# Hybrid DiT layer on one core: three attentions in one stage, PSUM banks shared by hand, and loads and splits moved ahead

## The chip, the cores and the metric

The kernel is one program on one core of a Trainium2 chip. The metric is device time in microseconds (us); lower is better. Engines are named as in the profile: PE (TensorE matmul), PEld (its weight loads), DVE (VectorE), ACT (ScalarE), POOL (GpSimd), SP (SyncE, which here only issues transfers). SPq, ACTq and POOLq are the sequencers of those engines.

## What is computed

One layer (DEPTH 1) over 512 latent tokens and 256 context tokens, 768 together, D_MODEL 2048, all float32. Cut to what matters:

```python
hn_lat = rmsnorm(h, norm1_g) * (1 + sc1) + sh1      # 512 tokens; hn_ctx likewise, 256 tokens
pc, pl = split(hn_ctx @ w_in), split(hn_lat @ w_in) # q_lat 512, kv_lat 256, k_rope 64, mLSTM q k v o 768 each, gates 8 + 8, NA q k v 512 each
q = rope(rmsnorm(q_lat) @ w_uq); k = rope(rmsnorm(kv_lat) @ w_uk); v = rmsnorm(kv_lat) @ w_uv
mla = softmax(q k^T * scale) v                      # 6 heads, 128 + 64 wide, values 128
ml  = mlstm_bidirectional(...)                      # 4 heads of 192, both directions, exponential gates
na  = softmax(q k^T * scale + bias) v               # 4 heads of 128; neighbourhood of 8 x 16 plus the context
h = h + g1 * (concat(mla, ml, na) @ w_out)          # 768 + 768 + 512 = 2048
h = h + g2 * conv_ffn(rmsnorm(h) * (1 + sc2) + sh2) # w_up, depthwise conv of 3, silu gate, w_down
return rmsnorm(h, final_norm_g)
```

## The kernel before, in words

Four parts follow one another: `stage_front` (norms, modulation, the projection by `w_in` in 43 column tiles), `stage_mix` (the three attentions), and `stage_tail` (output projection and ConvFFN). Each `nc.Block` ends in a join: no engine begins the next block before all have left this one. `stage_mix` has four blocks in turn: the MLA projections, the MLA softmax, the mLSTM, and the NA softmax. The big products of front and tail are made in three passes over operands split into a high and a low half (`x_hi`, `x_lo`, `f_hi`, `f_lo`): ACT copies the high half (L1639, L1612), DVE subtracts for the low one (L1745, L1715), PE multiplies (L1844).

**MLA projections** (`stage_mla`, L793 to L1023). SP loads the latent of the queries and the two norm gains (L797 to L799), the gate biases (L802), then the latent of keys and values and the rope inputs; ACT issues the three weight loads, `w_uq` first (L842 to L844); POOL loads the gate rows (L829). ACT scales the query latent by the gain (L847, four instructions), and PE waits for all four before its first product (L1003). Beside that, DVE and ACT turn the gates into rows (L894 to L930) that SP stores to the DRAM tensors `rrow` and `em`; DVE then rotates the queries (L933).

**MLA softmax** (`softmax_heads`, 6 heads x 4 query tiles = 24 units, tag `a`). Unit u: PE scores it (L1030), DVE takes the maximum (L1136, L1138), ACT the exponential (L1183), DVE the inverse of its sum (L1144), POOL multiplies (L1157). Two units later PE transposes it (L1105), ACT and DVE copy it out of PSUM (L1166, L1118), and once a head is complete PE multiplies by the values (L1089) and ACT stores the head to the DRAM tensor `mix` (L1173, L1175). While this runs SP loads the mLSTM operands (`prefetch`).

**mLSTM** (`stage_mlstm`, 4 heads x 6 key tiles = 24 units, tag `g`). For each unit SP loads a row of weights, repeated over the partitions, into one of 5 ring slots (L1265), once the values product of five units earlier is done; POOL adds the causal mask for four tiles of six (L1283), ACT takes the exponential (L1334), PE scores two units ahead (L1426), DVE multiplies score by weight (L1366, L1371), and PE multiplies by the values (L1447). After a head, ACT reads the sums out of PSUM (L1344), DVE makes and inverts the denominators (L1383, L1387, L1392), PE spreads them over the partitions (L1456), DVE scales (L1400), POOL joins the two directions and gates them (L1290, L1292), SP stores to `mix` (L1254). For heads 0 to 2 that is spread over the units of the next head; for head 3 it stands at the end of the block. The ACT queue opens this block by issuing the operands of NA: queries, keys, values, the window and eight slabs of bias (L1312 to L1319); POOL adds the window to the slabs after its masks of head 0 (L1300).

**NA softmax** (`stage_na`, 16 units, tag `c`) is the same `softmax_heads`; here DVE adds the bias out of the slab (L1127, L1129) and finds the maximum (L1133).

**Tail** (`stage_tail`). SP loads tile 0 of `w_out` (L1564), all of `mix` (L1569, 4 MB), tile 1, the residual `h` (L1571, 4 MB) and the conv weights. ACT splits 16 blocks of `mix` and tile 0, DVE follows with the low halves; then DVE waits for `h` and only after it takes the low half of tile 1. Product 0 waits block by block for `x_lo`, product 1 for `f_lo` of tile 1.

PSUM is held by names: each block takes its own tiles and gives them back.

## Time and profile before

| | |
|---|---|
| median of 3 runs | 2904.06 us (2904.06, 2904.89, 2895.7) |
| profiled execution | 2902.73 us, span of its instructions 2901.1 us, mean granted clock 0.964 |
| PE busy | 2699.4 us, 93% of the span, 12122 matmuls |
| DVE, ACT, POOL busy | 1197.9, 741.8, 192.9 us |
| DMA | 371.13 MB, mean 128 GB/s |
| first PE instruction of the MLA projections | 721.42 us |
| first score of the mLSTM, first values | 968.90 us, 990.36 us |
| first score of NA | 1132.30 us |
| first load of the tail, first product | 1216.22 us, 1237.70 us |

A busy PE is not a PE at its peak: the clock granted to it is one of two levels, and at the lower one the same matmul takes twice as long while its busy time reads the same share. The time to look for is therefore idle PE and PE at a clock below 1.00. The stretch of this change is about a fifth of the span, from 702 us (the last product of the front) to 1252 us (the second tile of the tail).

### The profile page before, as it was taken

The page shows a single profiled execution, that of the slowest core. Times are in us where ns is not written, and L with a number is a line of the kernel's source. Part 1 is how long each engine was busy: PE and PEld are TensorE (multiplying, and loading weights), DVE is VectorE, ACT ScalarE, POOL GpSimd, SP SyncE. Part 2 cuts the span into 40 slices and gives each one's busy share as a digit, 9 for nine tenths or more (in the row PEclk, how much of TensorE's full clock was granted, in tenths as well). Part 3 has the DMA queues.
Part 4 walks back from the last instruction along what each step waited for, and adds up shares of the span by engine and source line. Part 5 has one row for each costly group of instructions (what it writes and reads, how often), then busy time and mean ns, then how long its engine had stood idle before and what let it go on. Part 6 is the DMA issues. An engine that isn't in the chain of part 4 may idle for free.

```text
span 2901.1 us, 31111 instructions
## 1 busy us (share of the span) xinstructions
PE 2699.4 (93%) x12122; PEld 2088.8 (72%) x12122; DVE 1197.9 (41%) x1220; ACT 741.8 (26%) x822; POOL 192.9 (7%) x195
## 2 busy tenths in 40 slices
PE   5999999997999696599899999999999999999996
PEld 3788888885534243278678888888888888888785
DVE  5535434651622155343544433344333433334334
ACT  3222112221223121232333321223212322223221
POOL 1000000001033223200000000000000000000000
PEclk9999999998979798899999999999999999999998
DMA  9765555863050520242222222222232222322222
GB/s 354 272 245 209 218 197 214 316 242 126 11 114 12 155 83 16 96 168 87 73 101 87 101 90 99 102 95 101 81 113 87 101 97 90 103 96 98 82 90 98
DMA packets 98923, 371.13 MB, mean 128 GB/s; under 512 B 21920, under 2 KB 35280, under 8 KB 68360
## 3 DMA queue, kind: packets, MB, share of 16 engines
...
q14 instruction: 22, 0.18, 0.0%
HBM read 347.53 MB, written 22.79 MB: 128 GB/s over the span
## 4 chain that ended last, share of the span: by engine, by line
PE 56%; DVE 1%; DMA 1%; issue 0%; ACT 0%; DVEq 0%; SPq 0%; ACTq 0%
PE f_ps L1844 55%; PE f_ps L1857 1%; DMA mix_under_u<-mix 1%; DVE h L1833 0%; DVE f_lo L1715 0%; ACT f_hi L1612 0%; DVE f_square_sum L1830 0%; PE f_pn L1871 0%; DVE h L1732 0%; DVE f_square_sum L1739 0%; ACT f_val L1618 0%; ACT x_hi L1639 0%; PE f_pn L1890 0%; ACT f_val L1631 0%; DVE f_val L1726 0%
## 5 line engine op out<-in xcount | busy, mean ns | idle before, releaser
L1844 PE MATMUL f_ps<-x_hi,f_hi 128*128 128x512 f32 x1632 | 637.1, 390 | 29.1 <-DVE f_lo L1715 29.1
L1844 PE MATMUL f_ps<-x_lo,f_hi 128*128 128x512 f32 x1632 | 636.6, 390 | 0.0
L1844 PE MATMUL f_ps<-x_hi,f_lo 128*128 128x512 f32 x1632 | 636.5, 390 | 0.0
L1715 DVE TENSOR_TENSOR f_lo<-f_raw,f_hi 128x2048 fp32r<-128x2048 f32 (+1 forms) x167 | 340.1, 2037 | 105.8 <-ACT f_hi L1612 100.5
L1844 PEld LDWEIGHTS f_ps<-x_hi,f_hi 128*128 128x128 f32 x1632 | 307.3, 188 | 94.2 <-DVE f_lo L1715 25.5
L1612 ACT ACTIVATE f_hi<-f_raw 128x2048 fp32r<-128x2048 f32 (+1 forms) x168 | 286.2, 1703 | 280.0 <-PE f_ps L1844 280.0
L1844 PEld LDWEIGHTS f_ps<-x_lo,f_hi 128*128 128x128 f32 x1632 | 307.5, 188 | 64.0
L1844 PEld LDWEIGHTS f_ps<-x_hi,f_lo 128*128 128x128 f32 x1632 | 307.4, 188 | 64.1
L1844 PE MATMUL f_ps<-f_u_hi,f_hi 128*128 128x512 f32 x704 | 274.7, 390 | 4.9 <-DVE f_u_lo L1795 4.9
L1844 PE MATMUL f_ps<-f_u_hi,f_lo 128*128 128x512 f32 x704 | 274.4, 390 | 0.0
L1844 PE MATMUL f_ps<-f_u_lo,f_hi 128*128 128x512 f32 x704 | 274.3, 390 | 0.0
L542 PE MATMUL i_ps<-hn_hi,i_hi 128*128 128x512 f32 x608 | 240.5, 395 | 0.0
L542 PE MATMUL i_ps<-hn_hi,i_lo 128*128 128x512 f32 x608 | 239.7, 394 | 0.0
L542 PE MATMUL i_ps<-hn_lo,i_hi 128*128 128x512 f32 x608 | 238.5, 392 | 0.0
L1732 DVE SCALAR_TENSOR_TENSOR h<-f_ps,mod,h 128x512 f32 (+1 forms) x80 | 60.1, 751 | 339.2 <-PE f_ps L1844 339.2
L422 DVE TENSOR_TENSOR i_lo<-i_raw,i_hi 128x2048 fp32r<-128x2048 f32 x38 | 87.0, 2291 | 218.3 <-ACT i_hi L295 218.3
L1844 PEld LDWEIGHTS f_ps<-f_u_hi,f_hi 128*128 128x128 f32 x704 | 132.5, 188 | 32.7 <-issue 5.3
L1723 DVE SCALAR_TENSOR_TENSOR f_val<-f_ps,f_conv,f_val 128x511 f32<-128x511 f32 x44 | 33.0, 750 | 294.8 <-ACT f_val L1631 294.8
L1844 PEld LDWEIGHTS f_ps<-f_u_lo,f_hi 128*128 128x128 f32 x704 | 132.6, 188 | 27.6
L1844 PEld LDWEIGHTS f_ps<-f_u_hi,f_lo 128*128 128x128 f32 x704 | 132.4, 188 | 27.7
L434 DVE SCALAR_TENSOR_TENSOR i_ring<-i_ring,cs 128x2048 f32<-128x2048 f32 x60 | 138.2, 2346 | 0.0
L542 PEld LDWEIGHTS i_ps<-hn_hi,i_hi 128*128 128x128 f32 x608 | 114.2, 188 | 27.7 <-issue 1.7
...
## 6 DMA issues: line engine op xcount, KB each, us to landing
...
g_ring<-rrow SPq DMA_DIRECT2D x24, 256.0 KB, 3.4
...
```

Source lines behind the costliest of these rows:

```text
L422: nc.vector.tensor_tensor(w_lo[s][:, :, :], raw[s][:, :, :], w_hi[s][:, :, :].bitcast(F32), ALU.subtract).then_inc(lo_ok, 1)
L434: nc.vector.scalar_tensor_tensor(acc[g], ada[g % 2], col, acc[g], ALU.mult, ALU.add).then_inc(ada_ok, 1)
L542: mm = nc.tensor.matmul(pt[s][:, 0:SEQ], w[s][:, k, :], x[:, k, 0:SEQ], **flags)
L1612: nc.scalar.activation(w_hi[s][:, 0:kt, :], raw[s][:, 0:kt, :], ACT.Copy).then_inc(hi_ok, 1)
L1715: nc.vector.tensor_tensor(w_lo[s][:, 0:kt, :], raw[s][:, 0:kt, :], w_hi[s][:, 0:kt, :].bitcast(F32), ALU.subtract).then_inc(lo_ok, 1)
L1723: nc.vector.scalar_tensor_tensor(y[s][:, 1:SEQ], pt[s][:, 0:SEQ - 1], conv[:, col, 0:1].rearrange("p a b -> p (a b)"), y[s][:, 1:SEQ], ALU ...
L1732: nc.vector.scalar_tensor_tensor(ht, pt[s][:, :], mod[:, bass.ds(group * KT + m, 1), 0:1].rearrange("p a b -> p (a b)"), ht, ALU.mult, ALU ...
L1844: mm = nc.tensor.matmul(pt[s][:, :], w[s][:, k, :], v[:, c, :], start=(k == 0 and n == 0), stop=(k == len(slots) - 1 and n == 2))
L1857: mm = nc.tensor.matmul(pt[s][:, :], w[s][:, k, :], v[:, k, :], start=(k == 0 and n == 0), stop=(k == KT - 1 and n == 2))
```

## The change

The three attentions keep their arithmetic. What changes is where loads are issued, which blocks there are, and in which order some instructions stand.

**Early MLA operands.** The front's SP loads `w_uq` once the sums of the modulation are done, and after its last column tile the query latent and then the latent of keys and values; POOL loads the two gains at the start. They lie in place of the front's ring. The MLA block drops those five loads; its ACT waits for the query latent alone, and PE's first job waits for its four scaled pieces one by one.

**One block for three attentions** (`stage_heads`, new). MLA softmax, mLSTM and NA softmax are built by the functions `softmax` and `mlstm` as pieces for each engine and put into one block. One PSUM tile of eight banks is shared by hand: MLA scores in 0-1 and 2-3, transposes in 4-5, output in 6; mLSTM scores in 0, 1, 2, outputs in 3 to 6, spread in 7; NA scores in 0-1 and 3-4, transposes in 5-6, output in 2. The mLSTM constants and the first five ring slots are loaded during the MLA softmax; the first two mLSTM scores and exponentials stand among the last transposes of MLA. The operands of NA go to the SP queue, in 15 parts, two after each row load of units 6 to 13; POOL masks the slabs at head 2 instead of head 0. The end of mLSTM head 3 (floors, inverses, scaling, spreads) is taken into units 0 to 4 of NA, its gating to POOL after unit 5.

**NA.** Lag 3 instead of 2 (three buffers for the exponentials and for the normalised ones), the inverse one unit later; heads are not stored to `mix`: ACT writes `x_hi` and DVE `x_lo` straight from PSUM.

**Output projection prepared during NA.** SP loads tile 0 of `w_out` and the 12 `mix` blocks of MLA and mLSTM behind the last store; ACT splits tile 0 after unit 10 and 12 blocks after units 11 to 14, DVE takes the low half of tile 0 after unit 11 and of 6 blocks after units 12 to 14. The tail's SP loads tile 1, `h` and the conv weights; its DVE takes the remaining 6 low halves first. DVE still waits for `h` ahead of the low half of tile 1.

```diff
                 with sp.Fori(1, PAIRS) as i:
                     load(sp, 2 * i, 0)
                     load(sp, 2 * i + 1, 1)
+                sp.wait_ge(sums, 2)
+                sp.dma_start(lat["wq"][:, :, :], A["w_uq"].rearrange("(k p) n -> p k n", p=P)).then_inc(lat["w_ld"], 16)
+                for s in range(2):
+                    sp.wait_ge(*slot_free[NF + NB - NFB + 3 + s])
...
+                sp.dma_start(lat["ql"][:, :, :], proj[r:r + Q_LORA, 0:SEQ].rearrange("(k p) t -> p k t", p=P)
...
+                sp.dma_start(lat["kl"][:, :, :], proj[r:r + KV_LORA, :].rearrange("(k p) t -> p k t", p=P)
...
-                act.wait_ge(q_ld, 48)
+                act.wait_ge(q_ld, 16)
...
-                        pe.wait_ge(qg_ok, QK)
...
+                        if j == 0:
+                            pe.wait_ge(qg_ok, k + 1)
...
+                for n in range(SLOTS_R):
+                    two.load_rows(sp, n)
+
+                sp.wait_ge(one.o_ok, MLA_H)
+                sp.wait_ge(one.oe_ok, MLA_H)
+                two.load_floors(sp)
...
+                for n in range(SLOTS_R, two.UNITS):
+                    two.load_rows(sp, n)
+                    if n % KEYT == 4 and n // KEYT >= 2:
+                        two.put(sp, n // KEYT - 2, mix)
+                    if n >= SLOTS_R + 1:
+                        for dst, src, s in parts[2 * (n - SLOTS_R - 1):2 * (n - SLOTS_R)]:
+                            sp.dma_start(dst, src).then_inc(s, 16)
+                two.put(sp, ML_H - 2, mix)
+                two.put(sp, ML_H - 1, mix)
+                sp.dma_start(w_raw[:, :, :], A["w_out"][0:1, :, :, :].rearrange("o p k m -> (o p) k m")).then_inc(early["w_ld"], 16)
...
+                sp.dma_start(x_raw[:, 0:half, :], rows[:, 0:half, :]).then_inc(mix_ld[0], 16)
+                sp.wait_ge(two.stored, 16 * ML_H)
+                sp.dma_start(x_raw[:, half:LOADED, :], rows[:, half:LOADED, :]).then_inc(mix_ld[1], 16)
...
+                def to_mlstm(u):
+                    if u == 0:
+                        pe.wait_ge(ml_ld, 16 * (3 + KEYT))
+                        pe.wait_ge(one.e_ok, one.UNITS)
+                    two.score(pe, u)
+                one.tensor(pe, to_mlstm)
+                pe.wait_ge(one.oe_ok, MLA_H)
+                two.tensor(pe)
+
+                def after(u):
+                    if u in (3, 4):
+                        two.spread(pe, ML_H - 1, u - 3)
+
+                def ready(u):
+                    if u == 0:
+                        pe.wait_ge(na_ld, 16 * 6)
+                    if u == 1:
+                        pe.wait_ge(two.oe_ok, 4 * ML_H)
+                three.tensor(pe, None, after, ready)
...
             def _(sp):
-                load(sp, 0, 0, A["w_out"][0:1, :, :, :], KT)
-                sp.dma_start(mx[:, :, :], mix.rearrange("(k p) t -> p k t", p=P)).then_inc(mix_ld, 16)
                 load(sp, 1, 1, A["w_out"][1:2, :, :, :], KT)
                 sp.dma_start(h[:, :, :], A["xT"].rearrange("(k p) t -> p k t", p=P)).then_inc(x_ld, 16)
...
-                act.wait_ge(mix_ld, 16)
-                for k in range(KT):
-                    nc.scalar.activation(x_hi[:, k, :], mx[:, k, :], ACT.Copy).then_inc(mh_ok, 1)
-                    if k == 1:
-                        split_hi(act, 0, 0, 0, KT)
...
-                for k in range(KT):
+                for k in range(LOW_EARLY, LOADED):
                     dve.wait_ge(mh_ok, k + 1)
-                    nc.vector.tensor_tensor(x_lo[:, k, :], mx[:, k, :], x_hi[:, k, :].bitcast(F32),
+                    nc.vector.tensor_tensor(x_lo[:, k, :], x_raw[:, k, :], x_hi[:, k, :].bitcast(F32),
                                             ALU.subtract).then_inc(ml_ok, 1)
-                    if k == 1:
-                        split_lo(dve, 0, 0, KT)
```

How the order of instructions moves, at three places (row: line, operation, out<-in, shape). First ACT between the MLA softmax and the mLSTM, before (`a_` is MLA, `n_` the operands of NA, `g_ring` the weight rows):

```order
L1173 ACTIVATE a_out_4223<-a_o 128x512
L1175 DMA mix<-a_out_4223 128x512
L1166 ACTIVATE a_probT_4222<-a_t 128x4x128 x2
L1173 ACTIVATE a_out_4224<-a_o 128x512
L1175 DMA mix<-a_out_4224 128x512
L1080 UNCONDITIONAL_BRANCH
L1308 UNCONDITIONAL_BRANCH
L1312 DMA n_q<-proj 128x4x512
L1312 DMA n_k<-proj 128x4x768
L1313 DMA n_v<-vtok 128x6x512
L1314 DMA n_window<-in_window 128x64
L1319 DMA n_slab<-in_rpb 64x14x64 x8
L1334 ACTIVATE g_ring_5093<-g_ring_5093,l_ccol 128x512 x2
L1334 ACTIVATE g_ring_5094<-g_ring_5094,l_ccol 128x512 x2
```

The same place in the changed kernel; PSUM reads as `m_banks`:

```order
L1385 ACTIVATE a_probT_4239<-m_banks 128x4x128
L1215 ACTIVATE a_out_4244<-m_banks 128x512
L1217 DMA mix<-a_out_4244 128x512
L1519 ACTIVATE g_ring_3751<-g_ring_3751,l_ccol 128x512 x2
L1385 ACTIVATE a_probT_4239<-m_banks 128x4x128
L1519 ACTIVATE g_ring_3752<-g_ring_3752,l_ccol 128x512 x2
L1385 ACTIVATE a_probT_4239<-m_banks 128x4x128
L1215 ACTIVATE a_out_4245<-m_banks 128x512
L1217 DMA mix<-a_out_4245 128x512
L1519 ACTIVATE g_ring_3753<-g_ring_3753,l_ccol 128x128
L1519 ACTIVATE g_ring_3753<-g_ring_3753,l_ccol 128x512
```

The twelve transfers of NA and the ends of two blocks are gone from between the last MLA head and the first exponential of weights, and two units' exponentials stand ahead of that head.

Second, DVE between the mLSTM and NA, before (`c_` is NA, `g_dinv` the denominators of head 3, `g_num` its numerators):

```order
L1383 SCALAR_TENSOR_TENSOR g_dinv<-g_num,g_em 32x512 x2
L1387 TENSOR_TENSOR g_dinv<-g_dinv,g_num 32x512 x2
L1392 RECIPROCAL g_dinv<-g_dinv 32x512 x2
L1400 TENSOR_TENSOR g_num<-g_num,g_b 96x512 x4
L1244 UNCONDITIONAL_BRANCH
L1111 UNCONDITIONAL_BRANCH
L1127 SCALAR_TENSOR_TENSOR c_score_5809<-c_s,n_slab 128x512
L1129 TENSOR_SCALAR c_score_5809<-c_s 128x256
L1133 TENSOR_REDUCE c_negmax<-c_score_5809 128x1
```

In the changed kernel:

```order
L1343 SCALAR_TENSOR_TENSOR c_score_4262<-m_banks,n_slab 128x512
L1345 TENSOR_SCALAR c_score_4262<-m_banks 128x256
L1349 TENSOR_REDUCE c_negmax<-c_score_4262 128x1
L1548 SCALAR_TENSOR_TENSOR g_dinv<-g_num,g_em 32x512 x2
L1552 TENSOR_TENSOR g_dinv<-g_dinv,g_num 32x512 x2
L1343 SCALAR_TENSOR_TENSOR c_score_4263<-m_banks,n_slab 128x512
L1345 TENSOR_SCALAR c_score_4263<-m_banks 128x256
L1349 TENSOR_REDUCE c_negmax<-c_score_4263 128x1
L1557 RECIPROCAL g_dinv<-g_dinv 32x512
L1331 RECIPROCAL c_inv<-c_sum 128x1
L1343 SCALAR_TENSOR_TENSOR c_score_4262<-m_banks,n_slab 128x512
```

The bias of NA's first unit now stands ahead of the floors of head 3, and each inverse and each scaling behind the bias of a further unit.

Third, SP during the mLSTM, changed kernel (rows of weights `g_ring`, operands of NA between them; before, no `n_` row stood on this queue):

```order
L1467 DMA g_ring_3752<-rrow 128x512 x2
L1134 DMA n_q<-proj 128x4x512
L1134 DMA n_k<-proj 128x2x768
L1467 DMA g_ring_3753<-rrow 128x512 x2
L1134 DMA n_k<-proj 128x2x768
L1134 DMA n_v<-vtok 128x2x512
L1467 DMA g_ring_3754<-rrow 128x128
L1467 DMA g_ring_3754<-rrow 128x512
L1134 DMA n_v<-vtok 128x2x512 x2
L1467 DMA g_ring_3755<-rrow 128x256
L1467 DMA g_ring_3755<-rrow 128x384
```

Every row load from unit 7 to 14 now has two transfers of NA ahead of it on the same queue (the last has one).

## Rows read from the trace of the kernel before

**Rows 1.** The page: busy time (part 1) and the chain that ended last (part 4).

```profile
PE 2699.4 (93%) x12122; PEld 2088.8 (72%) x12122; DVE 1197.9 (41%) x1220; ACT 741.8 (26%) x822; POOL 192.9 (7%) x195
...
PE f_ps L1844 55%; PE f_ps L1857 1%; DMA mix_under_u<-mix 1%; DVE h L1833 0%; DVE f_lo L1715 0%; ACT f_hi L1612 0%; DVE f_square_sum L1830 0%; PE f_pn L1871 0%; DVE h L1732 0%; DVE f_square_sum L1739 0%; ACT f_val L1618 0%; ACT x_hi L1639 0%; PE f_pn L1890 0%; ACT f_val L1631 0%; DVE f_val L1726 0%
```

**Rows 2.** Windows: us, PE, PEld, DVE, ACT, POOL busy (x count), PEclk, DMA share, GB/s.

```profile
807.10:837.00 29.90, 29.90 (x47) 11.16 (x48) 6.19 (x14) 5.30 (x10) 7.45 (x4) 0.50 0.90 193
...
1106.60:1132.30 25.70, 4.13 (x5) 1.03 (x5) 12.03 (x10) 2.06 (x4) 8.73 (x7) 0.58 0.11 31
1132.30:1213.10 80.80, 60.41 (x208) 32.77 (x208) 38.69 (x80) 25.86 (x52) 35.29 (x16) 0.92 0.03 10
1213.10:1237.70 24.60, 0.00 (x0) 0.00 (x1) 3.64 (x4) 5.92 (x9) 0.00 (x0) 0.57 0.88 324
```

**Rows 3.** Waits, 940 to 1260 us: total us, times, longest us.

```profile
ACT g_ring L1334 <- issue: 30.7, 1, 30.7
...
PE f_ps L1844 <- DVE f_lo L1715: 24.6, 1, 24.6
```

**Rows 4.** Timeline at the start of the MLA projections: start us, us, engine, line, operation.

```profile
704.94 0.46 ACTq L842 DMA_DIRECT2D a_w_uq<-in_w_uq  x1
...
708.12 0.50 POOL L830 DMA_DIRECT2D l_rows<-proj  x1
...
718.72 2.56 ACT L847 ACTIVATE a_q_g_times<-a_q_lat,a_q_g 128x512 f32<-128x512 f32 x4 [16.30 <-DMA a_kv_g<-in_kvn]
719.97 0.72 DVE L898 TENSOR_SCALAR l_rows<-l_rows,l_gate_bias 36x768 f32<-36x768 f32 x1 [14.91 <-DMA l_gate_bias<-in_f_bias]
...
721.42 8.92 PE L1003 MATMUL a_pj<-a_q_g_times,a_w_uq 128*128 128x512 f32 x16 [19.64 <-ACT a_q_g_times L847]
...
757.20 0.69 DVE L933 TENSOR_TENSOR a_q_rope<-a_pj,a_rope 128x512 f32<-128x512 f32 x1 [4.77 <-PE a_pj L1007]
```

**Rows 5.** DMA issues, us to landing: gate rows; row loads, 955 to 1000 us, then overall.

```profile
l_rows<-proj POOLq DMA_DIRECT2D x4, 12.0 KB, 5.6
...
g_ring<-rrow SPq DMA_DIRECT2D x6, 256.0 KB, 11.5
...
g_ring<-rrow SPq DMA_DIRECT2D x24, 256.0 KB, 3.4
```

**Rows 6.** Timeline at the start of the mLSTM.

```profile
948.17 8.19 PE L1089 MATMUL a_o<-a_probT,a_v 128*128 128x512 f32 x12 [0.69 <-ACT a_probT L1166]
...
959.50 1.38 POOL L1275 MEMSET l_v<- 128x1536 f32 x1 [13.88 <-POOLq L1080]
...
960.82 0.96 POOL L1276 MEMSET g_dinv<- 128x1024 f32 x1
...
990.36 5.86 PE L1447 MATMUL g_o<-g_ring,l_v 128*128 128x512 f32 x8 [13.42 <-DVE g_ring L1366]
...
1023.59 3.60 PE L1447 MATMUL g_o<-g_ring,l_v 128*128 128x512 f32 x8
```

**Rows 7.** Timeline, end of the mLSTM and NA.

```profile
1112.76 6.55 DVE L1392 RECIPROCAL g_dinv<-g_dinv 32x512 f32<-32x512 f32 x2
...
1155.89 5.32 PE L1089 MATMUL c_o<-c_probT,n_v 128*128 128x512 f32 x12
...
1205.56 7.50 PE L1089 MATMUL c_o<-c_probT,n_v 128*128 128x512 f32 x12 [0.69 <-ACT c_probT L1166]
```

**Rows 8.** Timeline at the start of the tail.

```profile
1235.23 7.37 ACT L1639 ACTIVATE x_hi<-mix_under_u 128x512 fp32r<-128x512 f32 x14
...
1237.56 8.51 DVE L1745 TENSOR_TENSOR x_lo<-mix_under_u,x_hi 128x512 fp32r<-128x512 f32 x14
1237.70 0.79 PE L1844 MATMUL f_ps<-x_hi,f_hi 128*128 128x512 f32 x1 [24.65 <-DVE f_lo L1715]
...
1246.96 2.29 DVE L1715 TENSOR_TENSOR f_lo<-f_raw,f_hi 128x2048 fp32r<-128x2048 f32 x1 [0.34 <-DMA h<-in_xT]
...
1251.81 0.75 DVE L1732 SCALAR_TENSOR_TENSOR h<-f_ps,mod,h 128x512 f32<-128x512 f32 x1 [2.56 <-PE f_ps L1844]
```

More of the change, by code:

```diff
@@ L1052, in softmax_heads, with softmax @@
+class Engines:
+    pass
+def softmax(nc, arena, at, sem, tag, heads, score, v, scale, bias, ident, lag, s_ps, t_ps, o_ps):
     D = P
     UNITS = heads * QT
-    pr = [arena.at(f"{tag}_prob{n}", [P, TOK], at + 3072 * n) for n in range(2)]
-    pn = [arena.at(f"{tag}_normed{n}", [P, TOK], at + 6144 + 3072 * n) for n in range(2)]
-    pT = [arena.at(f"{tag}_probT{n}", [P, KEYT, SEQ], at + 12288 + 12288 * n) for n in range(2)]
-    o = [arena.at(f"{tag}_out{n}", [P, SEQ], at + 36864 + 2048 * n) for n in range(2)]
@@ L1490, in stage_tail @@
-def stage_tail(nc, A, out, sb, ps, sem, mix, ones, eps, mod, sc_ffn, gfcol):
+    f = Engines()
+    f.UNITS = UNITS
+    c_ld = f.c_ld = sem("g_consts_loaded")
+    e_ld = sem("g_floors_loaded")
+    r_ld = [sem(f"g_rows_loaded{n}") for n in range(SLOTS)]
+    z_ok = sem("g_zeroed")
+    mk_ok = sem("g_masked")
+    w_ok = sem("g_weight_done")
+    s_ok = sem("g_scored")
+    a_ok = sem("g_weighted_done")
+    v_ok = sem("g_unit_done")
+    oe_ok = f.oe_ok = sem("g_sums_read")
+    d_ok = sem("g_den_step")
@@ new lines, in mlstm, with weights @@
+    masks = 0
+    def weights(act, n):
+        nonlocal masks
+        h, st, s = n // KEYT, ORDER[n % KEYT], n % SLOTS
+        if st < QT:
+            masks += 1
+            act.wait_ge(mk_ok, masks)
+        else:
+            act.wait_ge(r_ld[s], 32 * (n // SLOTS + 1))
+        at = 0
+        for d in (1, 0):
+            w = SEQ if st >= QT else lat_widths(st)[1 - d]
+            nc.scalar.activation(ring[s][:, at:at + w], ring[s][:, at:at + w], ACT.Exp,
+                                 bias=ccol[:, st, 32 * d + h:32 * d + h + 1]).then_inc(w_ok, 1)
+            at += w
@@ new lines, in scalar, with read_sums @@
+    def scalar(act):
+        def read_sums(h):
+            act.wait_ge(v_ok, KEYT * (h + 1))
+            if h >= 1:
+                act.wait_ge(ha_ok, 2 * h)
+            for d in range(2):
+                for n in range(2):
+                    nc.scalar.activation(num[:, 2 * d + n, :], o_ps[d][n], ACT.Copy).then_inc(oe_ok, 1)
+        weights(act, AHEAD - 1)
+        for n in range(UNITS):
+            if n + AHEAD < UNITS:
+                weights(act, n + AHEAD)
+            if n % KEYT == KEYT - 1:
+                read_sums(n // KEYT)
@@ new lines, in finish, with products_done, score @@
+    def finish(dve, u):
+        h = ML_H - 1
+        if u == 0:
+            floors(dve, h)
+        elif u < 3:
+            invert(dve, h, u - 1)
+        elif u < 5:
+            scaled(dve, h, u - 3)
+    def products_done(n):
+        return 10 * (n // KEYT) + (1, 2, 4, 6, 8, 10)[n % KEYT]
+    def score(pe, n):
+        h, st = n // KEYT, ORDER[n % KEYT]
+        if n >= 3:
+            pe.wait_ge(a_ok, products_done(n - 3))
+        for a in range(2):
+            mm = nc.tensor.matmul(s_ps[n % 3], k[:, 2 * h + a, st * P:(st + 1) * P], q[:, 2 * h + a, :],
+                                  start=(a == 0), stop=(a == 1))
+        mm.then_inc(s_ok, 1)
@@ L1492, in stage_tail @@
+    f.load_rows, f.load_floors, f.put, f.gated, f.weights, f.finish = load_rows, load_floors, put, gated, weights, finish
+    f.score, f.spread = score, spread
+    f.tensor, f.vector, f.gpsimd, f.scalar = tensor, vector, gpsimd, scalar
+    return f
+def stage_tail(nc, A, out, ground, ps, sem, ones, eps, mod, sc_ffn, gfcol, early):
     UP = 2 * GT
```

938 lines of the change are left out of this document (486 added, 452 removed).

## Prediction

> **What bounds the kernel now.** The page first: PE is busy for 2699.4 us, 93% of the span, and the chain that ended last is mostly the tail's products [rows 1]. Work taken off DVE, ACT or POOL is therefore worth something only where PE stands still or runs at the lower clock. So I read the stretch of the change by windows [rows 2], and look for idle PE and for a granted clock near 0.50. Four places show it: the start of the MLA projections (19.64 us idle) [rows 4], the change from MLA to mLSTM, the change from mLSTM to NA (4.13 us busy of 25.7) and the change from NA to the tail (0.00 busy of 24.6) [rows 2]. The waits say what ends two of them: the first exponential of weights stood 30.7 us behind the ACT queue itself ("issue"), and the first product of the tail 24.6 us behind the split of the first weight tile [rows 3]. I take one term for each place, against the profiled execution of 2902.73 us; the median of the runs is 1.3 above it. A difference of 0.3% (8.7 us) is about what measurements of this kernel can tell from none.
>
> **Term 1, front to MLA: -14.6.** PE's first product is at 721.42, just after ACT began to scale the query latent at 718.72, which waited for a gain of 1 KB queued behind the latent [rows 4]. The block began at 704.9. With latent, `w_uq` and gains already there, ACT issues two loads (0.5 each, like the 0.46 of the row) and scales the first quarter (2.56/4 = 0.64): PE starts at about 706.8, 14.6 earlier. The front pays nothing: its SP queue is at its end there. Next in line is the gate chain on DVE. It began at 719.97 because of its biases and is done 4.77 before 757.20, at 752.4 [rows 4]. The gate rows are issued at 708.12 and land 5.6 later [rows 4, 5], at 713.7, so the chain is done by 746.1, against the rotation's new due time of 757.2 - 14.6 = 742.6. The 3.5 between are covered by the two PSUM tiles of the projections. Bounds: nothing lost, or 3.5 to 4 if that cover is not there. I take nothing, since the chain's middle part waits on ACT, which is freer too.
>
> **Term 2, MLA to mLSTM: -34.0.** Before: last values at 948.17 (8.19 long, at half clock), first weighted values at 990.36 and 5.86 long [rows 6]. After: the first two scores and exponentials stand among the last transposes, so those products may run at full clock, 5.32 [rows 7], starting 0.4 later for the inserted scores. Then ACT copies the head out (0.65, as it takes 0.64 for a like piece [rows 4]), POOL fills two buffers (1.38 + 0.96) [rows 6], PE makes one score (two matmuls of up to 0.79 at half clock [rows 8], 1.6, and 0.1 to begin) and the values: 948.6 + 5.3 + 0.65 + 2.35 + 1.7 = 958.6. That is 31.8 earlier, and at full clock they take 3.60 [rows 6] for 5.86: 2.2 more. Bounds: 3 less if both products stay at half clock (8.19 for 5.32), 1 more if the fills are hidden. Row slots: 5 are loaded during the MLA softmax, whose DMA is nearly idle in its second half. What the edit moves rather than removes is the load of the NA operands: 4.2 MB and eight slabs of 224 KB, 6.0 MB, now in the same queue as the rows for units 7 to 14. At the mLSTM's pace, (1106.6 - 990.4)/24 = 4.8 us per unit [rows 2, 6], that stretch lasts 39 us; with some 3 MB of rows it asks for 9 MB, 236 GB/s, below the 324 the queues carried at the start of the tail [rows 2]. A row is issued when the slot comes free, and needed about two units (9.7 us) later; it lands in 3.4 as a median, 11.5 among the operand burst [rows 5]. Bounds: 0, or 8 loads x (11.5 - 9.7) = 14. I take 0, since each row has at most two parts ahead of it, not twelve.
>
> **Term 3, from the end of the mLSTM to the start of the tail: -19.6.** Before, from 1106.6 to the first load of the tail at 1216.2 is 109.6. It consists of 25.7 in which DVE works 12.03 on head 3 and PE 4.13, of 80.8 for 16 NA units, and of 3.1 for the last copy and the join [rows 2]. After, DVE binds at the start: its 12.03, of which the inverses are 6.55 [rows 2, 7], and five units at 38.69/16 = 2.42 [rows 2], make 24.1. Units 5 to 15 go at the period of a head, 17.55 before (values at 1155.89, then one every 17.55, the last at 1205.56 being earlier because nothing follows it) [rows 7], and now longer by the inserted splits: on ACT one tile (1.9) and 12 blocks of 7.37/14 = 0.53, 8.2; on DVE 2.29, 6 x 8.51/14 = 3.6 and four head splits taken as 0.7, 8.7 in all [rows 8]. With lag 3 POOL's 35.29/16 = 2.2 per unit [rows 2] is hidden, and about half of the splits too: head period 19. So 24.1 + 11 x 19/4 = 76.3; the drain (inverse, normalising, transposes, 5.32 to 7.50 of values [rows 7], two head copies) adds 11.3, and the clock, 0.58 in that window before [rows 2], costs 2.4 in the first units. 90.0 against 109.6. Bounds: splits all hidden, 6 less; splits all serial, 15 more (a rival below).
>
> **Term 4, start of the tail to product 1: -13.6.** Before, DVE takes product 0 out at 1251.81 and PE goes on without a gap: 1251.8 - 1216.2 = 35.6 [rows 8]. Product 0 can start at once after; but product 1 needs the low half of tile 1, and DVE makes it after `h` landed (the row at 1246.96, [0.34 <-DMA h]) [rows 8]. Before `h` the queue carries 1 + 4 + 1 + 4 MB in 30.4 us, after it 1 + 4 MB. With 2.5 us until the first bytes (a row of 256 KB lands in 3.4 [rows 5], of which the bytes are under 1), 10.5 MB in 27.9 is 376 GB/s, and 5.24 MB takes 13.9 + 2.5 = 16.4. Then 0.3 and 2.29: product 1 at 19.0, 16.6 earlier. Product 0 is over before that, so PE idles 4 to 7 us and product 1 begins at half clock, as product 0 did (0.63 a matmul for 0.39 [rows 8]): +3. Bounds: 0 to +3 for that clock, and -2 if `h` comes faster alone.
>
> The remaining edits (gains on POOL's queue, masking of the slabs at head 2 instead of head 0, MLA's PSUM banks by hand) lie beside work of other engines: POOL is busy 7% of the span [rows 1]. Masking takes about 8 us of POOL in a stage where it has pauses of that size; if it did not fit, it would delay one mask of head 3 by that and no more than 4 us of it would reach PE.
>
> **Sum.** -14.6 - 34.0 - 19.6 - 13.6 = -81.8; 2902.73 - 81.8 = 2820.9, and with the 1.3 to the median **2822**. Everything behind product 1 is unchanged.
>
> **Rivals.** *A, the clock.* For 30 us at the start of the MLA softmax PE was busy without pause and was granted 0.50 [rows 2]. If the other timing of its start gives it the full clock there, half of that time goes: -15, 2807. For it speaks only that the loads beside it (share 0.90) come in another pattern; against it, that the block boundary ahead of it is unchanged. The Trainium skill (TensorE: Matmul & The Clock Gate, Part 1: The HAM clock gate) has the clock rise after a stretch of sustained activity; by that rule this window should not exist and the sum would be 2807; the trace disagrees. Chance 0.12.
>
> *B, in-order splits.* DVE and ACT each have one order; if each inserted split delays the next unit in full, term 3 is worse by about 15: 2837. For it: DVE's bias frees the score bank and is on the chain of every unit. Against: ACT is busy 25.86 of 80.8 [rows 2]. Chance 0.18.
>
> *C, rows late.* The rows for units 7 to 14 land as in the burst: +14 by the bound above, 2836; with part of them, 2831. For it: the 11.5 of the row [rows 5]. Chance 0.12. The Trainium skill (DMA: Bandwidth & Descriptors, Issuing engines are not separate DMA queues) says that transfers from any queue run on the same engines and interleave. By that rule the queue that issues the NA operands makes no difference to the rows, only how many bytes are under way beside one; the 11.5, measured with the operands on ACT's queue, agrees.
>
> *D, slower.* If the row loads became the pace of the mLSTM altogether, each of the 19 loads behind the first five would have to stall PE by more than 81.8/19 = 4.3 us, so land after 14 us and not after 3.4. Then it is 2904 and above, at 15.5 us about 2930. Only eight of them have anything ahead of them. Chance 0.02.
>
> *E, the change does not do what it says*: early splits gain nothing as `h` is late whatever is prepared, and term 4 keeps its 35.6, 2836. Against it: the bytes ahead of `h` are halved. Chance 0.04.
>
> **Numbers.** Forecast case (all terms as costed, within their small bounds: 2808 to 2832) 0.52, A 0.12, B 0.18, C 0.12, D 0.02, E 0.04. The range holds the forecast case, most of A, and B, C and E up to two of them together: 2802 to 2846. Faster by over 0.3% in every case but D: 0.97; within 0.3% 0.01; slower 0.02.
>
> **What would show it.** First MLA product within 2.5 us of the start of its block (term 1); last MLA head to first weighted values under 6 us (term 2); from the last values of the mLSTM to the first load of the tail 90 us, no idle PE over 8 us in it, and a distance between NA values near 19 (term 3); product 1 at 19 us behind that load, waiting for the low half and DVE for `h` (term 4). Wrong would be: DVE's wait ended by gates in the MLA projections, "g_ring <- DMA" waits of over 5 us that reach PE in the mLSTM, or NA values over 22 us apart.

## The result, and the profile after

The changed kernel takes 2851.61 us (median of 4 runs, 2849.53 to 2856.57), the kernel before 2899.88 us (median of 4, three of them those shown above). The ratio is 0.9837, with a 95% interval of 0.9810 to 0.9864: 47 us or 1.6% faster, where 2822 (82 us faster) was forecast and 2802 was to 2846 the range. The profiled execution took 2849.53 us with a span of 2847.9, which is 53.2 us shorter than the 2901.1 of the kernel before.

The page of the changed kernel, parts 1, 2 and 4:

```profile
PE 2715.9 (95%) x12122; PEld 2087.1 (73%) x12122; DVE 1196.4 (42%) x1220; ACT 739.6 (26%) x818; POOL 192.7 (7%) x197
...
PEclk9999999999989998999999999999999999999998
...
PE f_ps L1997 57%; PE f_ps L2010 1%; DMA h<-in_xT 1%; DVE h L1986 0%; DVE f_lo L1870 0%; DVE f_square_sum L1983 0%; ACT f_hi L1772 0%; DVE h L1887 0%; DVE f_square_sum L1894 0%; ACT f_val L1778 0%; PE f_pn L2043 0%; PE f_pn L2024 0%; ACT f_val L1791 0%; DVE f_val L1881 0%; DVE f_val L1878 0%
```

PE is busier by 16.5 us than in [rows 1] although the matmuls are the same 12122. Idle time went away, as forecast, but part of it came back as busy time. The chain still names little but the tail's products (L1844, now L1997), with 57% of a shorter span.

The places of the four terms, in the timeline of the changed kernel (start us, us, engine, line, operation). The MLA projections and the first MLA score:

```profile
708.58 10.16 PE L1031 MATMUL a_pj<-a_q_g_times,a_w_uq 128*128 128x512 f32 x16 [5.03 <-ACT a_q_g_times L874]
...
798.84 2.05 PE L1072 MATMUL m_banks<-a_k_nope,a_q_nope 128*128 128x512 f32 x2 [4.79 <-PEq L828]
```

The last values of MLA, and the first scores and values of the mLSTM:

```profile
936.54 5.42 PE L1292 MATMUL m_banks<-a_probT,a_v 128*128 128x512 f32 x12 [0.69 <-ACT a_probT L1385]
...
945.08 2.02 PE L1612 MATMUL m_banks<-l_q,l_k 96*128 96x512 f32 x4 [3.13 <-issue]
946.89 5.28 PE L1637 MATMUL m_banks<-g_ring,l_v 128*128 128x512 f32 x8
```

The last values of the mLSTM, NA's second to fourth scores, and NA's four values products:

```profile
1059.83 2.33 PE L1637 MATMUL m_banks<-g_ring,l_v 128*128 128x128 f32 x8
...
1066.90 5.60 PE L1078 MATMUL m_banks<-n_k,n_q 128*128 128x512 f32 x12 [3.45 <-ACT g_num L1530]
...
1097.08 5.32 PE L1292 MATMUL m_banks<-c_probT,n_v 128*128 128x512 f32 x12
...
1115.23 5.32 PE L1292 MATMUL m_banks<-c_probT,n_v 128*128 128x512 f32 x12
...
1134.96 5.32 PE L1292 MATMUL m_banks<-c_probT,n_v 128*128 128x512 f32 x12
...
1144.79 5.42 PE L1292 MATMUL m_banks<-c_probT,n_v 128*128 128x512 f32 x12 [0.69 <-ACT c_probT L1385]
```

The start of the tail, and product 1:

```profile
1151.84 0.35 SPq L1726 DMA_DIRECT2D f_raw<-in_w_out  x1
...
1152.04 0.47 PE L1997 MATMUL f_ps<-x_hi,f_hi 128*128 128x512 f32 x1 [1.83 <-PEq L1099]
...
1168.74 2.29 DVE L1870 TENSOR_TENSOR f_lo<-f_raw,f_hi 128x2048 fp32r<-128x2048 f32 x1 [12.61 <-DMA h<-in_xT]
...
1171.09 0.79 PE L1997 MATMUL f_ps<-x_hi,f_hi 128*128 128x512 f32 x1 [7.89 <-DVE f_lo L1870]
```

Each term against these rows, always from one event to the next:

| stretch | before | after | difference | forecast |
|---|---|---|---|---|
| start of the MLA block to its first product (term 1) | 16.5 | 1.9 | -14.6 | -14.6 |
| first product to first MLA score | 85.7 | 90.3 | +4.6 | 0 |
| first MLA score to first weighted values (term 2) | 183.3 | 148.1 | -35.2 | -31.8 |
| from there to the end of the mLSTM's values | 116.2 | 115.3 | -0.9 | -2.2 |
| end of the mLSTM to the tail's first load (term 3) | 109.6 | 89.7 | -19.9 | -19.6 |
| first load to product 1 (term 4) | 35.6 | 19.3 | -16.3 | -16.6, and +3 for the clock |
| **product 1 to the end of the span** | **1649.3** | **1676.8** | **+27.5** | **0** |

(Product 1 of the kernel before is put at 1251.8, where DVE reads product 0, as the prediction did [rows 8]; PE began it 0.2 us earlier. The front's own last product ended 1.8 us later in this execution, at 703.5 for 701.8; PE's instructions there are the same ones.) At the start of product 1 the changed kernel is 80.7 us ahead. Then it loses a third of that in a part of the program where the diff touches no instruction, in kind, shape or order.

Windows of 400 us in the middle of the tail, PE alone (us, busy and count, PEclk, DMA share, GB/s), kernel before:

```profile
1900.00:2300.00 400.00, 400.00 (x1766) 1.00 0.28 96
```

The same window of the changed kernel:

```profile
1900.00:2300.00 400.00, 400.00 (x1740) 1.00 0.27 95
```

PE is busy throughout and at full clock in both, with nothing to wait for; but 1740 matmuls start where 1766 did. The busy share can't show this, since a matmul that takes longer is busy longer. By 26/1740 = 1.5% of the 1636 us that PE is busy from product 1 on, this is 24 of the 27.5 us; most of the rest is product 1's start at the lower clock (10 matmuls at 0.43 between starts for 0.23: 2.0).

Finer, the changed kernel's timeline around one change of weight tile:

```profile
1519.80 0.39 PE L1997 MATMUL f_ps<-x_lo,f_hi 128*128 128x512 f32 x1
...
1523.20 0.39 PE L1997 MATMUL f_ps<-x_lo,f_hi 128*128 128x512 f32 x1
...
1524.82 0.39 PE L1997 MATMUL f_ps<-x_hi,f_lo 128*128 128x512 f32 x1
...
1528.32 0.40 PE L1997 MATMUL f_ps<-x_hi,f_lo 128*128 128x512 f32 x1
```

Fifteen steps lie between the first and the second row, and between the third and the fourth: 3.40/15 = 226.7 ns and 3.50/15 = 233.3 ns a step. The change from one pace to the other comes with the tile: **slot 0 of the two weight buffers runs at 227 ns, slot 1 at 233.** In the kernel before both run at 227.

What differs between the slots is where they lie. The diff also gives the tail a memory plan by hand, which the excerpt further up leaves out and the prediction took no notice of:

```diff
-        h = sb("h", [P, KT, SEQ], F32, ctx)
-        x_hi = sb("x_hi", [P, KT, SEQ], F32R, ctx)
...
-        w_hi = [sb(f"f_hi{s}", [P, KT, P], F32R, ctx) for s in range(2)]
-        w_lo = [sb(f"f_lo{s}", [P, KT, P], F32R, ctx) for s in range(2)]
...
+        u_hi = ground.at("f_u_hi", [P, SLOTS, SEQ], 0, F32R)
+        raw = [early["raw"], ground.at("f_raw1", [P, KT, P], 24576)]
+        w_hi = [early["w_hi"], ground.at("f_hi1", [P, KT, P], 32768, F32R)]
```

### The profile page after: what moved, and what is told of

It reads as the page before. It is cut to its first block, busy times and chain, and to the rows that moved or that the text cites. A ratio compares the mean times of both kernels' runs of the same rounds, so it can differ in the third digit from the quotient of the medians.

```text
span 2847.9 us, 31082 instructions
## 1 busy us (share of the span) xinstructions
PE 2715.9 (95%) x12122; PEld 2087.1 (73%) x12122; DVE 1196.4 (42%) x1220; ACT 739.6 (26%) x818; POOL 192.7 (7%) x197
## 4 chain that ended last, share of the span: by engine, by line
PE 57%; DVE 1%; DMA 1%; issue 0%; ACT 0%; DVEq 0%; SPq 0%
PE f_ps L1997 57%; PE f_ps L2010 1%; DMA h<-in_xT 1%; DVE h L1986 0%; DVE f_lo L1870 0%; DVE f_square_sum L1983 0%; ACT f_hi L1772 0%; DVE h L1887 0%; DVE f_square_sum L1894 0%; ACT f_val L1778 0%; PE f_pn L2043 0%; PE f_pn L2024 0%; ACT f_val L1791 0%; DVE f_val L1881 0%; DVE f_val L1878 0%
## 5 line engine op out<-in xcount | busy, mean ns | idle before, releaser
L1997 PE MATMUL f_ps<-x_hi,f_hi 128*128 128x512 f32 x1632 | 641.3, 393 | 14.1 <-DVE f_lo L1870 12.3
L1997 PE MATMUL f_ps<-x_hi,f_lo 128*128 128x512 f32 x1632 | 643.3, 394 | 0.0
L1997 PE MATMUL f_ps<-x_lo,f_hi 128*128 128x512 f32 x1632 | 641.9, 393 | 0.0
L1997 PEld LDWEIGHTS f_ps<-x_hi,f_hi 128*128 128x128 f32 x1632 | 307.7, 189 | 84.8 <-DVE f_lo L1870 8.3
L1997 PEld LDWEIGHTS f_ps<-x_lo,f_hi 128*128 128x128 f32 x1632 | 307.8, 189 | 71.0
L1997 PEld LDWEIGHTS f_ps<-x_hi,f_lo 128*128 128x128 f32 x1632 | 307.4, 188 | 68.5
L1997 PE MATMUL f_ps<-f_u_hi,f_hi 128*128 128x512 f32 x704 | 277.5, 394 | 4.9 <-DVE f_u_lo L1948 4.9
L1997 PE MATMUL f_ps<-f_u_lo,f_hi 128*128 128x512 f32 x704 | 276.7, 393 | 0.0
L1997 PE MATMUL f_ps<-f_u_hi,f_lo 128*128 128x512 f32 x704 | 276.3, 393 | 0.0
L1997 PEld LDWEIGHTS f_ps<-f_u_hi,f_hi 128*128 128x128 f32 x704 | 132.9, 189 | 35.4 <-issue 5.5
L1997 PEld LDWEIGHTS f_ps<-f_u_hi,f_lo 128*128 128x128 f32 x704 | 132.3, 188 | 30.9
L1997 PEld LDWEIGHTS f_ps<-f_u_lo,f_hi 128*128 128x128 f32 x704 | 132.5, 188 | 29.3
```

The source lines that it names most:

```text
L1997: mm = nc.tensor.matmul(pt[s][:, :], w[s][:, k, :], v[:, c, :], start=(k == 0 and n == 0), stop=(k == len(slots) - 1 and n == 2))
```

## Experiments

The theory from here on (A): the pace of these matmuls depends on how the byte offset (within a partition) of the weight tile stands to that of the operand that streams past it. Rivals: (B) slot 1 is slow by its place, high and low weights 98 KB apart; (C) other engines' traffic in the tail does it. Beside that, runs on terms 1, 3 and 4.

**e1: all tiles alike modulo 2048, in the changed kernel.**

```diff
-T_W0 = 48768
-T_X = 142976
+T_W0 = 50816
+T_X = 145024
...
-        u_hi = ground.at("f_u_hi", [P, SLOTS, SEQ], 0, F32R)
+        u_hi = ground.at("f_u_hi", [P, SLOTS, SEQ], 1664, F32R)
...
-        w_hi = [early["w_hi"], ground.at("f_hi1", [P, KT, P], 32768, F32R)]
+        w_hi = [early["w_hi"], ground.at("f_hi1", [P, KT, P], 34432, F32R)]
```

and all others by 1664 or 2048.

> The changed kernel, with the tail's tiles moved by up to 2048 bytes so that all operands of its products lie at the same offset modulo 2048 (in the changed kernel f_u_hi and f_hi1 lie 128 bytes off the others modulo 512; in the kernel before all were alike). Theory A, relative alignment: matmuls of slot 1 come every 227 ns as those of slot 0 do, and not every 233 (median), the mean of a tail product's three kinds falls from 393 to 390 ns, and the time falls by 22 to 25 us, to about 2827. Rival B, place: slot 1 is slow because its high and low weights lie 98 KB apart (they still do): nothing changes, 2850. Rival C, other engines' traffic in the tail: nothing changes.

Measured 2828.77 us, ratio to the kernel before 0.9740 (0.9704 to 0.9776) against 0.9837 for the change as it is. The window of e1:

```profile
1900.00:2300.00 400.00, 400.00 (x1766) 1.00 0.28 97
```

1766 again, as before the change. The weights of slot 1 still lie 98 KB apart and the traffic is the same, so B and C fall. From product 1 to the end of the span e1's trace takes 1653.9 us, 22.9 less than the changed kernel's.

**e2: the kernel before, `f_hi1` alone moved by 128 bytes.**

```diff
+        for n, (into, name, pad) in enumerate(((w_hi, "f_hi0", 0), (w_hi, "f_hi1", 32), (w_lo, "f_lo0", 96), (w_lo, "f_lo1", 0))):
+            if pad:
+                sb(f"f_pad{n}", [P, pad], F32, ctx)
```

A pad is counted in elements of 4 bytes: 128 bytes ahead of `f_hi1`, and 384 ahead of `f_lo0`, which puts all that follows back in line modulo 512.

> The kernel before, with only f_hi1 (high half of the weights in slot 1) moved by 128 bytes and everything behind it by 512. Theory A: its slot 1 products slow from 227 ns to 230 to 235 ns between starts, slot 0 stays; 51 output and up products of 48 matmuls and 32 down products of 33, by 6 ns, are 21 us: about 2921 against 2900. Rival B: 2900, no change, since the two halves lie 17 KB apart as before. Rival C: no change.

Measured 2928.46 us, ratio 1.0089 (1.0057 to 1.0121): 28 us slower from one pad. The window:

```profile
1900.00:2300.00 400.00, 400.00 (x1739) 1.00 0.28 97
```

The loss of the change is made anew in a kernel that has nothing else of it: 1739 matmuls against 1740.

**e5 and e6: other offsets, in the kernel before** (pads of the same kind).

> The kernel before with other offsets of the tail's weight tiles, modulo 512 and relative to x_hi, x_lo and f_u: slot 0 high and low halves both +128, slot 1 high half +256, low half 0. If the offset between weights and moving operand counts, all three kinds of slot 0 are slow (230 to 235 ns). If the offset between the two weight halves counts, slot 0 stays at 227. If the pattern repeats every 256 bytes slot 1 stays at 227; if only every 512, it is slow like the 128 case, 232 to 235.

> The kernel before, high half of slot 0 moved by 64 bytes, high half of slot 1 by 32. If any offset modulo 512 costs, both are slow; if the cost begins at 128, both stay at 227 ns and the time is that of before.

One run each: 2925.14 and 2942.22 us; the kernel before beside them 2900.61. The windows, e5:

```profile
1900.00:2300.00 400.00, 400.00 (x1742) 1.00 0.28 97
```

and e6:

```profile
1900.00:2300.00 400.00, 400.00 (x1727) 1.00 0.27 94
```

**e9: the kernel before, `x_lo` and `f_u_lo` moved by 128 bytes.**

> The kernel before, with x_lo and f_u_lo moved by 128 bytes against x_hi, f_u_hi and all weights. Theory A, refined by e5 and e6 to modulo 256: a matmul is slow when the weight tile that is loaded beside it and its moving operand lie apart modulo 256. Then only one kind of three is slow, the one that streams x_lo (232 to 235 ns), or this one and a neighbour, and the others stay at 227; the sum over the three is 680 + 6 to 12 ns in both slots. If all three are slow in both slots (above 696), the offsets of all operands count together and the two-operand account is too simple.

One run, 2949.23 us against 2901.3 before, the slowest of all. Its window:

```profile
1900.00:2300.00 400.00, 400.00 (x1716) 1.00 0.27 93
```

and the groups of its output and up products (busy us, mean ns of one), each 390 in the kernel before:

```profile
L1848 PE MATMUL f_ps<-x_hi,f_hi 128*128 128x512 f32 x1632 | 649.9, 398 | 29.0 <-DVE f_lo L1719 29.0
L1848 PE MATMUL f_ps<-x_lo,f_hi 128*128 128x512 f32 x1632 | 645.7, 396 | 0.0
L1848 PE MATMUL f_ps<-x_hi,f_lo 128*128 128x512 f32 x1632 | 641.6, 393 | 0.0
```

The table puts the six layouts together. A step is the mean distance between the starts of successive matmuls in the trace, over the 51 output and up products of a slot without their first and last; the three kinds are high times high, high weights times low, low weights times high.

| kernel | bytes off the rest, modulo 512 | steps in slot 0, ns | steps in slot 1, ns |
|---|---|---|---|
| before, e1 | none | 226.7 226.7 226.7 | 226.7 226.7 226.7 |
| changed | `f_hi1` (128) | 226.8 226.8 226.7 | 232.5 232.5 235.0 |
| e2 | `f_hi1` (128) | 226.7 226.7 226.7 | 232.5 232.5 235.0 |
| e5 | slot 0 both halves 128, `f_hi1` 256 | 232.4 232.4 232.4 | 226.7 226.7 226.7 |
| e6 | `f_hi0` 64, `f_hi1` 32 | 227.6 234.9 232.3 | 232.0 230.8 233.4 |
| e9 | `x_lo` 128 | 235.9 234.1 230.0 | 235.9 234.1 230.0 |

The down products fit. In the changed kernel `f_u_hi` lies where `f_hi1` does, 128 bytes off `f_hi0`, `f_u_lo` and the low weights; their steps are 232.5, 225.9 and 228.3 ns in slot 0 and 230.6, 233.6 and 230.0 in slot 1 (means without the lowest and highest tenth), and 226.5 to 226.9 in both slots in e1.

Three things follow. An offset of 256 costs nothing in the output and up products of e5's slot 1 (its down products take 228.0, 226.7 and 227.3), one of 128, 64 or 32 does: as far as these offsets show, the pattern repeats every 256 bytes. What counts is the relation and not the address itself: by the sizes allocated ahead of them and the shift of 1664, all tiles of e1 together lie 160 bytes further on, modulo 256, than those of the kernel before, at the same pace. And it is not the two weight halves among themselves, for in e5's slot 0 they lie alike and are slow against `x`. But the account by pairs is too simple. e9 was to slow one kind or two and slowed all three; `f_hi1` alone also slows the step in which the aligned `f_lo1` is loaded beside the aligned `x_lo`. A misplaced tile costs its neighbours in the order too. That the relative offsets set the pace is shown by e1 and e2, by taking the loss away and by making it; why they do is left open. The offsets 32, 64 and 256, and the moved `x_lo`, rest on one run each.

**e3: DVE waits for `h` only behind the low half of tile 1.**

```diff
-                dve.wait_ge(x_ld, 16)
-
                 def out_pair(i):
                     split_lo(dve, 2 * i + 1, 1, KT)
+                    if isinstance(i, int):
+                        dve.wait_ge(x_ld, 16)
```

> The changed kernel, DVE's wait for h moved behind the low half of tile 1 of w_out. If h bounds product 1 (term 4), product 1 starts when tile 1 is split, at 11 to 12 us behind the tail's first load instead of 20.9, without PE falling to half clock: 8 to 10 us less, 2841. If the DMA engines are the bound anyway (tile 2 comes behind h), the gain moves to a wait ahead of product 2 and is 3 us or less.

Measured 2842.36 us, 9.3 below the changed kernel, ratio 0.9795 (0.9759 to 0.9831); this interval still overlaps that of the changed kernel, so the size rests on the traces and on e4. In its timeline the low half of tile 1 follows its high half at once, 8 us behind the first load where it was 16.9:

```profile
1149.64 0.35 SPq L1726 DMA_DIRECT2D f_raw<-in_w_out  x1
...
1155.77 1.92 ACT L1772 ACTIVATE f_hi<-f_raw 128x2048 fp32r<-128x2048 f32 x1 [7.13 <-DMA f_raw<-in_w_out]
...
1157.72 2.29 DVE L1870 TENSOR_TENSOR f_lo<-f_raw,f_hi 128x2048 fp32r<-128x2048 f32 x1 [3.79 <-ACT f_hi L1772]
```

Product 1 follows product 0 with no fall of the clock, 11.0 us behind its start where it was 19.1. Of the gain 1.7 us come back, as PE's wait ahead of product 2 for the low half of tile 2.

**e4: e1 and e3 together.**

> Both: aligned tiles and the later wait for h. The two are independent by my account: 24 + 9 less, about 2818. If less than 25 comes together, one of them acts through the other.

Measured 2817.42 us, ratio 0.9712 (0.9679 to 0.9745): 34 us below the changed kernel and 83 below the one before, the fastest version. The two parts add up, within the noise: 22.8 + 9.3 = 32.

**e7: the early MLA loads undone** (in e1: `w_uq` and both latents loaded in the MLA block again, the gains still early).

```diff
-                sp.dma_start(lat["wq"][:, :, :], A["w_uq"].rearrange("(k p) n -> p k n", p=P)).then_inc(lat["w_ld"], 16)
...
+                act.dma_start(wq[:, :, :], A["w_uq"].rearrange("(k p) n -> p k n", p=P)).then_inc(w_ld, 16)
```

> The aligned kernel (e1), with the loads of w_uq and of the two latents back at the start of the MLA block (the two gains stay early). Term 1 says that the first product waits for the query latent and w_uq again: 9 to 14 us behind the start of the block instead of 1.9, so 7 to 12 us at that place. Rival: the clock gives half of it back, since a longer idle time is followed by one stretch at half clock and not two (in the changed kernel the projections took 4.6 us longer than before): 3 to 8 us in all, 2832 to 2837.

Measured 2834.83 us against 2828.77 for e1: 6 us, with intervals that overlap (ratios 0.9777, 0.9755 to 0.9798, and 0.9740, 0.9704 to 0.9776). Its timeline:

```profile
703.33 0.39 SPq L822 DMA_DIRECT2D a_q_lat<-proj  x1
...
716.48 0.50 PEld L1026 LDWEIGHTS a_pj<-a_q_g_times,a_w_uq 128*128 128x128 f32 x2 [16.72 <-DMA a_w_uq<-in_w_uq]
```

The first product comes 13.2 us behind the block's first transfer, waiting for `w_uq` alone, 11.3 later than in the changed kernel. How much of that lasts hangs on the clock behind it. The first 19.9 us of the projections and the first 29.9 of the MLA scores (windows as in [rows 2]), changed kernel:

```profile
708.50:728.40 19.90, 19.82 (x57) 11.37 (x58) 9.02 (x8) 12.17 (x14) 8.03 (x22) 0.67 0.56 160
798.80:828.70 29.90, 29.86 (x60) 11.26 (x60) 7.60 (x17) 5.61 (x11) 8.81 (x4) 0.64 0.90 189
```

The first 19.9 us of the projections before (its scores are in [rows 2]):

```profile
721.40:741.30 19.90, 19.88 (x68) 11.22 (x69) 11.19 (x10) 11.57 (x12) 2.37 (x6) 0.91 0.35 87
```

And both windows in e3, whose instructions there are those of the changed kernel:

```profile
704.79:724.69 19.90, 19.90 (x68) 11.13 (x69) 9.00 (x8) 13.12 (x15) 7.95 (x22) 0.90 0.57 160
790.70:820.60 29.90, 29.90 (x47) 11.13 (x48) 6.19 (x14) 5.30 (x10) 7.59 (x4) 0.50 0.89 190
```

Changed kernel against before, PE does 57 matmuls in the projections for 68, and 60 at the start of the scores for 47. It looks as if the shorter idle time (5.0 us for 19.6) had cost clock in the one place and brought it in the other. But e3 has the short idle time with the clock of the kernel before. All traces:

| instructions | PE idle before, us | traces | matmuls and clock, projections | matmuls and clock, scores | first product to first weighted values |
|---|---|---|---|---|---|
| changed | 5.0 | changed, e1, e4 | 57 or 58, 0.67 to 0.68 | 60 or 61, 0.64 | 238.2 to 238.4 |
| changed | 5.0 | e3, e4b, e8, e10 | 67 or 68, 0.88 to 0.90 | 47, 0.50 | 243.0 to 243.4 |
| e7 | 16.3 | e7 | 68, 0.91 | 47, 0.50 | 239.8 |
| before | 19.6 | before, e5 | 68, 0.91 | 47, 0.50 | 269.0, 269.1 |
| before | 19.8 to 19.9 | e2, e6 | 59, 0.70 to 0.71 | 47, 0.50 | 274.6, 274.5 |
| before | 19.9 | e9 | 59, 0.70 | 61, 0.64 | 267.3 |

So the same instructions behind the same idle time are granted one clock or another from execution to execution, and 5 to 7 us between two traces in these stages can be the clock's alone. The first weighted values of e7 come 256.1 us behind the front's last product, against 243.4 in e1 and 248.0 to 248.5 in e3, e4b, e8 and e10: the early loads are worth 8 to 13 us at that place. At product 1 e7 is 5.2 behind e1, because e1's mLSTM was granted less clock (119.9 us for 112.2, where the other traces with its instructions take 112.6 to 115.4). The 6 us of the times fit, but they don't settle the value.

**e8: nothing of the output projection prepared during NA** (in e1: tile 0 and the 12 blocks loaded and split in the tail).

```diff
+                load(sp, 0, 0, A["w_out"][0:1, :, :, :], KT)
+                sp.dma_start(x_raw[:, 0:LOADED, :], mix.rearrange("(k p) t -> p k t", p=P)[:, 0:LOADED, :]).then_inc(mix_ld, 16)
                 load(sp, 1, 1, A["w_out"][1:2, :, :, :], KT)
```

> The aligned kernel (e1), with tile 0 of w_out and the 12 blocks of mix loaded and split at the start of the tail, as before, and nothing of it during NA. Term 4 says that h lands about 11 us later (4 MB more ahead of it) and product 0 has to wait some 16 us; term 3 that NA gains 4 to 6 us, its values coming every 17.6 us and not every 19. Together 5 to 10 us slower than e1, 2834 to 2839. If the splits in NA cost more than they save (rival B), it is no slower or faster than e1.

Measured 2836.51 us against 2828.77: 7.7 slower, within the expectation, but again with overlapping intervals (ratio 0.9788, 0.9760 to 0.9817). Its timeline at the start of the tail:

```profile
1147.42 0.35 SPq L1702 DMA_DIRECT2D f_raw<-in_w_out  x1
1147.83 0.43 SPq L1707 DMA_DIRECT2D x_under_low<-mix  x1
...
1166.26 0.79 PE L1982 MATMUL f_ps<-x_hi,f_hi 128*128 128x512 f32 x1 [20.48 <-DVE f_lo L1853]
...
1175.73 2.29 DVE L1853 TENSOR_TENSOR f_lo<-f_raw,f_hi 128x2048 fp32r<-128x2048 f32 x1 [2.96 <-DMA h<-in_xT]
```

PE stands 20.5 us and product 1 gets its low half 28.3 us behind the first load, 11.4 later than in the changed kernel. From the end of the mLSTM to that first load e8 takes 86.6 us, e1 88.4, and the changed kernel, e3, e4 and e4b 89.2 to 89.7: the splits cost NA 2 to 3 us.

**e10 and e4b: lag 2 in NA, and e4 once more beside it.**

```diff
-        three = softmax(nc, arena, NSM_AT, sem, "c", NA_H, na_score, na["v"], NA_SCALE, na_bias, ident, 3,
+        three = softmax(nc, arena, NSM_AT, sem, "c", NA_H, na_score, na["v"], NA_SCALE, na_bias, ident, 2,
```

> e4 with lag 2 in NA instead of 3 (two buffers of exponentials and of normalised rows, the inverse in its own unit). My reason in term 3, that lag 3 hides POOL's 2.2 us, would make lag 2 slower: in the kernel before, with lag 2, values came every 17.55 us, with lag 3 and no splits every 18.2 to 19.4 (e8). So if lag 3 helps only the first five units, 0 to 4 us slower than e4; if it is only a longer way round, 0 to 5 us faster; 6 us slower or more would show that lag 3 carries NA.

> e4 once more, on the same chip and in the same rounds as e10, so that the two can be compared directly: 2817 us within 5, the tail's matmuls again every 227 ns in both slots.

Measured 2826.27 us for lag 2 (ratio 0.9737, 0.9711 to 0.9763) and 2821.79 for e4b (0.9723, 0.9700 to 0.9746); the intervals overlap, so the 4.5 us are not settled by the times. The values products, e10:

```profile
1095.31 5.32 PE L1292 MATMUL m_banks<-c_probT,n_v 128*128 128x512 f32 x12
...
1114.41 5.32 PE L1292 MATMUL m_banks<-c_probT,n_v 128*128 128x512 f32 x12
...
1134.26 5.32 PE L1292 MATMUL m_banks<-c_probT,n_v 128*128 128x512 f32 x12
...
1150.39 6.89 PE L1292 MATMUL m_banks<-c_probT,n_v 128*128 128x512 f32 x12 [0.69 <-ACT c_probT L1385]
```

and e4b:

```profile
1097.90 5.32 PE L1292 MATMUL m_banks<-c_probT,n_v 128*128 128x512 f32 x12
...
1116.07 5.32 PE L1292 MATMUL m_banks<-c_probT,n_v 128*128 128x512 f32 x12
...
1135.80 5.32 PE L1292 MATMUL m_banks<-c_probT,n_v 128*128 128x512 f32 x12
...
1145.63 5.42 PE L1292 MATMUL m_banks<-c_probT,n_v 128*128 128x512 f32 x12 [0.69 <-ACT c_probT L1385]
```

The second and third product come as soon with lag 2 (18 to 20 us apart in both), the last one 6 us later behind the third, and at the lower clock for a part. From the end of the mLSTM to the tail's first load e10 takes 95.0 us, e4b 89.7. So by these two traces lag 3 does not hide a pace set by POOL in the middle of NA, as I had it; it helps at the end, where the last transposes stand behind the inserted splits.

## Why the prediction was wrong

**The step that failed is the sentence "Everything behind product 1 is unchanged."** It was read from the instructions: order, shapes and counts are the same there. But the change moved every tile of the tail in memory, and the pace of its 7,104 matmuls hung on that: +24.4 us by the windows, 22.8 by the times of e1. The prediction compared instructions where the diff also had addresses. With that loss taken away, e1's 2828.77 is 7 us from the forecast of 2822 and inside its range. No rival had it either; all five concerned waits and the clock up to product 1.

**Terms 1 to 4** came out close: -14.6, -35.2, -19.9 and -16.3 at their own places against -14.6, -31.8, -19.6 and -16.6. Some of that is luck. Term 1 was right at its place, and the gate chain, which I had looked to as next in line, cost PE nothing. Term 2 was right where it was made: from the end of the last MLA head's values to the first weighted values it is 4.9 us for 34.0 before, and 4.7 was forecast. But no term had the clock of the long stretches between these places: in this trace 4.6 us came back in the projections. Term 2 was 3.4 better, since the MLA scores had the higher clock earlier, a part of rival A. Neither belongs to the change: in four other traces of the same instructions the projections give nothing back, and the first MLA score to the first weighted values takes 157.1 to 157.3 us, a gain of 26 and not of 35. Both stretches together fell from 269.0 to 238.3 us here and would have fallen to 243 there; forecast were 31.8 less.

**Term 3** came to its number with a wrong reason. The prediction says that about half of the splits' 17 us would show; the sum held only 11/4 x (19 - 17.55) = 4.0 for them. They cost NA 2 to 3 us (e8); but the head period without them is 18 to 19.4 us (e8's products come at 1092.96, 1112.38, 1130.54), not 17.55. And lag 3 saves at the end and not per unit (e10).

**Term 4** held, the start of product 1 at the lower clock included (2.0 for 3): product 1 waited for `h` by way of DVE's order, 12.6 us on DVE and 7.9 on PE, where 4 to 7 were forecast. e3 shows that the wait itself bought nothing.

**Rivals.** B (serial splits, +15) is refuted by e8. C (rows late, +14): from 944 to 1000 us the full rows landed with this median:

```profile
g_ring<-rrow SPq DMA_DIRECT2D x12, 256.0 KB, 5.3
```

and PE's waits from 940 to 1062 us name no row (POOL and ACT did wait for rows, 52.7 and 24.1 us in all, but PE's waits have other enders):

```profile
PE m_banks L1637 <- ACT g_num L1530: 6.6, 3, 2.8
```

The landing is 5.3 us with the operands of NA on the same queue, between the 3.4 and the 11.5 of [rows 5]. The rule that the prediction cites, that all queues run on the same engines (the Trainium skill, DMA: Bandwidth & Descriptors, Issuing engines are not separate DMA queues), fits: spread out over eight units, the same bytes on another queue delay the rows less than the burst did. A came in part, in some executions and not in others (table at e7). D and E did not come about.
